# Attention output projection split into two halves by input, the latent half issued inside the differential attention

## The chip, the cores and the metric

The kernel runs on one core of a Trainium2 chip. The metric is the device time of one execution in microseconds (us). Before the change the median of three runs is 2091.11 us, between 2088.5 and 2091.54 us.

The core has a matrix engine (TensorE, PE in the profile), a vector engine (VectorE, DVE), a scalar engine (ScalarE, ACT), GpSimd (POOL) and a queue engine (SyncE, SP). Each runs its own list of instructions in order, and they wait for each other by semaphores. Matrix products land in PSUM, eight banks of 128 x 512 floats, called `banks` in the rows.

## The reference

Two layers of an encoder over 512 prompt rows and 32 sample rows (R = 544 rows together), width 2048. What matters here is the first layer:

```python
o_a = _diff_attention(qa, k_all.reshape(b, sk, H_A, 2, DQK), v_all, lam, q_chunk, k_chunk)   # 8 heads x 128
o_a = _rmsnorm(o_a, g_subln, SUBLN_EPS) * (1.0 - lam_init)
o_lat = _mla_attention(q_lat, q_pe, ckv_all, kpe_all, q_chunk, k_chunk)
o_b = jnp.einsum('bshc,chv->bshv', o_lat, w_uv)                                             # 8 heads x 128
o = jnp.concatenate([o_a.reshape(b, s, W_A), o_b.reshape(b, s, W_B)], axis=-1) * jax.nn.silu(gate)
return o @ w_out, new_rows
...
x = x + gate * y
```

The output projection `o @ w_out` takes 2048 inputs, of which the last 1024 come from the latent attention and the first 1024 from the differential attention. Layer 1 (a pooling mixer with its own projections) and a final norm follow.

## The kernel before

Data are kept transposed: 128 features on the partitions, 544 rows along the free dimension, so an activation of width 2048 is 16 slices of 128 x 544 (index k). Every float32 value that enters a large product is split into a rounded upper part and the remainder (`w_hi`, `w_lo`, `h_hi`, `h_lo`), and a product is three matmuls: hi x hi, hi x lo, lo x hi. Each is done for two column halves of 272 rows. One output tile of a projection (128 outputs) therefore takes 16 x 3 x 2 = 96 matmuls of 128 x 272 (`big_tile`, `tile_products`); 8 of the 16 slices take 48.

The program is a fixed sequence written by hand: layer 0 input projections, latent attention, differential attention, the norm of its heads, the output projection, then layer 1. Each engine has its own block, and loops that must match are written once in each. The tile counter g (G_OUT is the first tile of the output projection) numbers the weight tiles; SP loads tile g into slot g % 2 of `w_raw`, `split` on DVE (L1390) makes `w_hi` and `w_lo` from it, and PE waits for `split_ready`.

**Differential attention.** 36 units are taken in steps w (`d_unit`): nine to a pair of heads, 8 blocks of 128 queries with 1, 2, 3, 4, 4, 3, 2, 1 key blocks (w % 9 = 0 to 7) and one unit of the sample rows (w % 9 = 8). A unit goes PE scores (`d_scores`), DVE maximum (L1660, or L1656 for the sample rows), ACT exponential (L1241, L1234), DVE reciprocal, ACT scaling of the second map (L1256) one step later, DVE combination (L1687) two steps later, PE transposes (`d_turn`, L935) three steps later, then ACT upper part (`ptd_hi`, L1263) and DVE remainder (`ptd_lo`, L1709). In the step d_last + 4 the products with the values follow (`d_values`, 12 matmuls, and `d_sample_values`). Score banks are 0 to 3, two for even and two for odd steps; PE may run at most two steps ahead of the exponential. Turns and transposed values take banks 4 and 5 in turn, value products bank 6 and sample rows bank 7.

**Heads' norm.** ACT squares the eight heads, PE sums them over the partitions, ACT and DVE take the root and its reciprocal for 8 rows, PE spreads them over the partitions (`sel_row` products), DVE scales each head, and ACT and DVE split it into `h_hi` and `h_lo`. PE fills the wait for the reciprocal with the latent half (k = 8 to 15) of one projection tile, G_OUT.

**Output projection.** 16 tiles. For each, DVE also computes one tile of the layer 1 modulation (`ada_tile`: two multiply-and-reduce instructions over 128 x 2048, L1433), ACT loads the modulation weights of the tile after next from its own queue, evicts the tile from PSUM times the gate (`gated`, L1302), DVE adds it to `x` (`update`, L1744), ACT squares it, POOL adds the square to `ssq` (L634), and DVE splits the weights of the tile after next (L1395, L1396). `x` is read again from memory at the end of the heads' norm.

## Time and profile before

| | |
|---|---|
| runs before (three) | 2088.5, 2091.11, 2091.54 us |
| profiled execution | 2090.51 us, span 2088.7 us, mean granted TensorE clock 0.928 |
| PE / DVE / ACT / POOL busy | 1859.8 / 1278.0 / 406.5 / 174.2 us |
| differential attention | from 1010 to 1179 us of the span |
| heads' norm | 1179 to about 1217 us |
| output projection to the last addition to x | about 1217 to 1401 us |
| layer 1 and the final norm | 1401 to 2088.7 us |
| DMA | 307.05 MB, mean 147 GB/s |

The profile gives busy time of each engine, tenths of it in 40 slices of 52.2 us, the chain of work that ended last, and groups of instructions by line. Ends of matmuls are modelled; the distance between the starts of two matmuls is a better measure of what one costs. The granted clock is a share of 2.4 GHz.

### The profile page before, as it was taken

What the parts mean: (1) busy time and instruction counts of PE and PEld (TensorE: products, weight loads), DVE (VectorE), ACT (ScalarE), POOL (GpSimd) and SP (SyncE); (2) the same over time, 40 slices, a digit from 0 to 9 for tenths busy, and PEclk for the clock granted to TensorE, in tenths of its full rate; (3) what the DMA queues carried; (4) which work ended last, traced back from release to release, by engine and by line L of the source; (5) the groups of instructions that cost most, each with busy time, mean ns of one, the idle gap of its engine ahead of it and who ended that gap; (6) DMA issues with size and microseconds to landing.
All of it is one profiled execution on the core that took longest, in us unless ns stands there. A gap on an engine that the chain in (4) does not pass through costs nothing.

```text
span 2088.7 us, 32490 instructions
## 1 busy us (share of the span) xinstructions
PE 1859.8 (89%) x13182; PEld 1707.9 (82%) x13182; DVE 1278.0 (61%) x1598; ACT 406.5 (19%) x863; POOL 174.2 (8%) x101
## 2 busy tenths in 40 slices
PE   4539999999999978997767799987999999999995
PEld 0109999999999966776655599987999999999995
DVE  4898677677877653553455678887334444583444
ACT  1241000000000112332344421113111111131111
POOL 2770000000600000000000011110000000001110
PEclk8879999999999999998666799997999999999997
DMA  9565555445655432116221064431322333452222
GB/s 390 219 230 186 200 196 213 183 187 209 238 201 209 162 106 61 56 32 197 73 61 57 26 287 173 182 127 56 118 102 107 105 124 112 160 192 98 80 80 85
DMA packets 77395, 307.05 MB, mean 147 GB/s; under 512 B 11416, under 2 KB 19784, under 8 KB 49440
## 3 DMA queue, kind: packets, MB, share of 16 engines
q1 hardware_dynamic: 55792, 218.56, 28.6%
q10 hardware_dynamic: 20912, 86.71, 11.6%
q0 software_dynamic: 640, 1.10, 0.1%
q8 instruction: 32, 0.52, 0.1%
q14 instruction: 19, 0.16, 0.0%
HBM read 278.10 MB, written 28.24 MB: 147 GB/s over the span
## 4 chain that ended last, share of the span: by engine, by line
PE 74%; DVE 14%; ACT 4%; DMA 3%; issue 2%; POOL 2%; DVEq 0%; SPq 0%; ACTq 0%; POOLq 0%
PE banks L646 73%; DVE banks L1433 2%; POOL ssq L609 2%; DMA w_more<-in_w_ada_pe 1%; ACT pxd L1241 1%; DMA d_raw<-pool_d_scratch 1%; DVE std L1660 1%; DVE w_lo L1396 1%; DVE h_lo L378 1%; DMA w_adr<-in_w_ada_dve 1%; DVE rstd L1375 1%; DVE x L1854 1%; DVE ptd_lo L1709 0%; ACT px L1185 0%; DVE pt_lo L1602 0%
## 5 line engine op out<-in xcount | busy, mean ns | idle before, releaser
L646 PE MATMUL banks<-h_hi,w_hi 128*128 128x272 f32 x3712 | 774.4, 290 | 36.2 <-DVE h_lo L1414 15.1
L646 PE MATMUL banks<-h_hi,w_lo 128*128 128x272 f32 x3712 | 772.7, 290 | 0.0
L646 PE MATMUL banks<-h_lo,w_hi 128*128 128x272 f32 x3712 | 770.1, 289 | 0.0
L646 PEld LDWEIGHTS banks<-h_hi,w_hi 128*128 128x128 f32 x3712 | 588.0, 190 | 41.6 <-issue 19.0
L646 PEld LDWEIGHTS banks<-h_lo,w_hi 128*128 128x128 f32 x3712 | 588.0, 190 | 0.0
L646 PEld LDWEIGHTS banks<-h_hi,w_lo 128*128 128x128 f32 x3712 | 584.4, 190 | 0.0
L1433 DVE CUSTOM_DVE_ANT_0 banks<-w_adr,cond_b 128x2048 f32<-128x2048 f32 x160 | 387.0, 2419 | 18.9 <-DMA w_adr<-in_w_ada_dve 15.7
L1396 DVE TENSOR_TENSOR w_lo<-w_raw,w_hi 128x2048 fp32r<-128x2048 f32 x117 | 299.4, 2559 | 4.0
L1395 DVE CAST w_hi<-w_raw 128x2048 fp32r<-128x2048 f32 x117 | 145.2, 1241 | 225.1 <-PE banks L646 216.9
L634 POOL TENSOR_TENSOR ssq<-ssq,stage 128x544 f32<-128x544 f32 x32 | 48.1, 1502 | 1261.3 <-ACT stage L1054 1261.3
L1131 ACT ACTIVATE stage<-banks 128x544 f32<-128x544 f32 x48 | 30.2, 628 | 519.4 <-PE banks L646 519.4
L1744 DVE TENSOR_TENSOR x<-x,stage 128x544 f32 (+1 forms) x32 | 23.2, 726 | 136.6 <-ACT stage L1302 136.3
L1790 DVE TENSOR_TENSOR w<-u_ext 128x573 f32<-128x573 f32 x16 | 12.1, 756 | 138.8 <-ACT u_ext L1323 138.8
L1302 ACT ACTIVATE stage<-banks,mod 128x272 f32<-128x272 f32 (+2 forms) x96 | 32.5, 409 | 287.4 <-PE banks L646 163.6
L646 PE MATMUL banks<-w_more,cond_t 128*2 128x512 f32 x80 | 42.1, 682 | 35.1 <-DMA w_more<-in_w_ada_pe 21.0
L646 PEld LDWEIGHTS banks<-w_more,cond_t 128*2 128x2 f32 x80 | 6.9, 92 | 69.2 <-issue 42.9
L646 PE MATMUL banks<-w_raw,cond_t 128*2 128x512 f32 x48 | 30.1, 786 | 35.1 <-DMA w_raw<-in_w_ada_pe 35.1
L935 PE MATMUL banks<-id_t,pxd 128*128 128x128 f32 x80 | 21.4, 382 | 41.1 <-DVE pxd L1687 27.0
L646 PEld LDWEIGHTS banks<-w_raw,cond_t 128*2 128x2 f32 x48 | 4.4, 101 | 58.7 <-DMA w_raw<-in_w_ada_pe 32.5
L935 PEld LDWEIGHTS banks<-id_t,pxd 128*128 128x128 f32 x80 | 11.8, 184 | 45.4 <-DVE pxd L1687 29.1
L646 PE MATMUL banks<-cq,wq 128*128 128x272 f32 x128 | 32.9, 412 | 15.4 <-DVE cq L1531 9.0
L646 PEld LDWEIGHTS banks<-cq,wq 128*128 128x128 f32 x128 | 24.8, 199 | 22.2 <-issue 17.2
(288 smaller groups left out, 1675.9 us busy)
## 6 DMA issues: line engine op xcount, KB each, us to landing
w_adr<-in_w_ada_dve ACTq DMA_DIRECT2D x60, 1024.0 KB, 4.9
w_raw<-in_w_z SPq DMA_DIRECT2D x32, 1024.0 KB, 6.2
w_raw<-in_w_pin SPq DMA_DIRECT2D x32, 1024.0 KB, 4.8
w_adr<-in_w_ada_dve SPq DMA_DIRECT2D x20, 1024.0 KB, 4.9
w_raw<-in_w_gate SPq DMA_DIRECT2D x16, 1024.0 KB, 6.1
w_raw<-in_w_out SPq DMA_DIRECT2D x16, 1024.0 KB, 4.9
w_raw<-in_w_pout SPq DMA_DIRECT2D x16, 1024.0 KB, 4.8
w_more<-in_w_ada_pe SPq DMA_DIRECT2D x10, 1024.0 KB, 7.2
```

What stands on the lines that cost most here:

```text
L378: ins = eng.scalar_tensor_tensor(out=h_lo[:, k, r], in0=x[:, k, r], scalar=mod[:, c, k:k + 1], in1=h_hi[:, k, r].bitcast(F32), op0=ALU.add ...
L609: pool.tensor_tensor(ssq[:], ssq[:], (stage[:, 0], rstd[:])[k % 2], ALU.add).then_inc(sq_added, 1)
L634: pool.tensor_tensor(ssq[:], ssq[:], stage[:, s], ALU.add).then_inc(sq_added, 1)
L646: return pe.matmul(out, lhsT, rhs, start=start, stop=stop)
L935: m = pe.transpose(PS[:, 4 + j % 2, b * P:(b + 1) * P], pxd[:, w % 3, 0, b * P:(b + 1) * P], id_t[:])
L1131: act.activation(rows(stage[:, s]), acc[slot], func).then_inc(acc_free[slot], 1)
L1241: ins = act.activation(pxd[:, w % 3, e, 0:n], PS[:, 2 * (w % 2) + e, 0:n], ACT.Exp, bias=std[:, w, 2 + e:3 + e], scale=DIFF_SCALE, accum_o ...
L1302: ins = act.activation(stage[:, s, r], PS[:, 2 * slot + bank, cols], ACT.Identity, scale=mod[:, c, bass.ds(2 * t + (gate_tile + s), 1)])
L1395: vchain(dve, dve.tensor_copy(w_hi[:, slot], w_raw[:, slot]))
L1396: dve.tensor_tensor(w_lo[:, slot], w_raw[:, slot], w_hi[:, slot].bitcast(F32), ALU.subtract).then_inc(split_ready, 1)
L1433: ins = dve.tensor_tensor_reduce(ada_junk, w_adr[:, slot], cond_b[:, c, :], 1.0, 0.0, ALU.mult, ALU.add, ada_acc[:, c:c + 1])
L1744: dve.tensor_tensor(at(x, t2 + k), at(x, t2 + k), stage[:, slot], ALU.add).then_inc(x_new, 1)
```

## The change

The output projection becomes two series of half tiles. The latent half (inputs 1024 to 2047) of tiles 0 to 12 goes into the steps w = 0 to 38 of the differential attention, three steps to a tile, with 3, 3 and 2 of its 8 slices; tiles 13, 14 and 15 are put around the heads' norm. Each result is evicted by ACT times the gate, added to its slice of the input `x` by POOL, and written by ACT's queue to a scratch buffer in memory. The other half of each tile follows where the projection was, and adds to the `x` read back from that buffer. Weights are loaded in halves, and their upper part is now made by ACT (128 x 1024) instead of DVE (128 x 2048). The jobs of banks 4 and 5 are laid out in one table that now holds the value products too, which leaves banks 6 and 7 to the latent half.

```diff
+            def latent_half(n, ks):
+                g = G_OUT + n
+                if 0 in ks:
+                    pe.wait_ge(split_ready, g - G_KPE + 2)
+                    pe.wait_ge(acc_free[(g - 1) % 2], turn_of(g + 1))
+                for k in ks:
+                    m = half_products(6, g, k, HEADS + k, k == 0, k == HEADS - 1)
+                if HEADS - 1 in ks:
+                    m.then_inc(mm_done, 1)
             for w in range(D_UNITS + DLAG + 1):
                 if w < D_UNITS:
                     d_scores(w)
+                if w > DLAG and (w - DLAG - 1) % 9 == 8:
+                    d_sample_values((w - DLAG - 1) // 9)
                 for h in range(HEADS):
                     if w == v_step(h):
                         d_values_in(h)
-                if DLAG <= w < D_UNITS + DLAG:
-                    d_turn(w - DLAG)
+                if w < 3 * IN_STEPS:
+                    latent_half(w // 3, chunk_of[w % 3])
                 for h in range(HEADS):
                     if w == d_last(h) + DLAG + 1:
                         d_values(h)
-                if w - DLAG - 1 >= 0 and (w - DLAG - 1) % 9 == 8:
-                    d_sample_values((w - DLAG - 1) // 9)
+                if DLAG <= w < D_UNITS + DLAG:
+                    d_turn(w - DLAG)
+            latent_half(13, range(HEADS))
...
+            latent_half(14, range(HEADS))
+            latent_half(15, range(4))
...
# ACT
+            def half_hi(g, t2=0, t=0):
+                act.wait_ge(raw_in[g % 2], 16 * t + 16 * (g // 2 + 1 - ADA_PE // 2))
+                act.wait_ge(mm_done, t2 + (g - 1))
+                act.activation(half_slots(g)[0], w_raw[:, g % 2, 0:D // 2], ACT.Copy).then_inc(w_upper, 1)
+            def store_half(n):
+                act.wait_ge(x1_added, n + 1)
+                act.dma_start(x1_scr[n], x_half[n % 2][:]).then_inc(x1_out[n % 2], 16)
+            def evict_half(n):
...
+                for bank, cols, r, c in parts(R):
+                    ins = act.activation(y_half[n % 2][:, r], PS[:, 6 + bank, cols], ACT.Identity,
+                                         scale=mod[:, c, 2 * KT + n:2 * KT + n + 1])
+                ins.then_inc(acc_free[g % 2], 1)
...
+                if w < 3 * IN_STEPS and w % 3 == 2:
+                    if w // 3:
+                        store_half(w // 3 - 1)
+                    evict_half(w // 3)
+                if w % 3 == 0 and w and w // 3 + 1 <= IN_STEPS:
+                    half_hi(G_OUT + w // 3 + 1)
# POOL
+            for n in range(KT):
+                pool.wait_ge(x1_in[n % 2], 16 * (n // 2 + 1))
+                pool.wait_ge(x1_ev, n + 1)
+                pool.tensor_tensor(x_half[n % 2][:], x_half[n % 2][:], y_half[n % 2][:], ALU.add).then_inc(x1_added, 1)
# DVE
+            def half_lo(g, t2=0, t=0):
+                hi, lo = half_slots(g)
+                dve.wait_ge(w_upper, t2 + (g - G_OUT + 1))
+                dve.tensor_tensor(lo, w_raw[:, g % 2, 0:D // 2], hi.bitcast(F32), ALU.subtract).then_inc(split_ready, 1)
...
+                if w % 3 == 1 and w > 3 and w // 3 + 1 <= IN_STEPS:
+                    half_lo(G_OUT + w // 3 + 1)
...
+            with dve.Fori(0, KT // 2 - 2) as t:
+                dv.loop(t, 4)
                 for s in range(2):
                     ada_tile(ADA_P0 + ADA_P1 + s, 2 * t, t)
-                    update(G_OUT + s, 2 * t, t, 1, s, s)
-                    split(G_OUT + s + 2, 2 * t, t)
+                    update(G_O2 + s, 2 * t, t, 1, s, s)
+                    half_lo(G_O2 + s + 2, 2 * t, t)
```

In the new loop of the projection, `gated` on ACT does `half_hi` of the tile after next between the eviction and the square. SP issues the half loads, the slices of x, and the loads of heads and caches step by step in one list, and the condition vectors for `ada_tile` are loaded at the end of the attention steps instead of at the end of the heads' norm.

**PE, around step w % 9 = 7.** Before, the turn of unit w - 3 (L935) stands ahead of the value products (the rows with `ptd_hi` and `vr_hi`), which the sample scores (`kcs`) follow:

```order
L646 MATMUL banks<-kd_hi,qd_hi 128x128 x2
L646 MATMUL banks<-kd_hi,qd_lo 128x128 x2
L646 MATMUL banks<-kd_lo,qd_hi 128x128 x2
L646 MATMUL banks<-maskk_t,maskq_t 128x64 x2
L935 MATMUL banks<-id_t,pxd 128x128 x4
L646 MATMUL banks<-ptd_hi,vr_hi 128x512
```

Now the same scores, a chunk of three slices (L712 with `h_hi`, `w_hi`; the lower part of a latent half tile also lies in the tile called `w_hi`), the value products, and only then the turn (L1012):

```order
L712 MATMUL banks<-kd_hi,qd_hi 128x128 x2
L712 MATMUL banks<-kd_hi,qd_lo 128x128 x2
L712 MATMUL banks<-kd_lo,qd_hi 128x128 x2
L712 MATMUL banks<-maskk_t,maskq_t 128x64 x2
L712 MATMUL banks<-h_hi,w_hi 128x272 x2
...
L712 MATMUL banks<-h_hi,w_hi 128x272 x2
L712 MATMUL banks<-ptd_hi,vr_hi 128x512
...
L712 MATMUL banks<-ptd_lo,vr_hi 128x128
L1012 MATMUL banks<-id_t,pxd 128x128 x4
L712 MATMUL banks<-kcs,qds 32x272
```

The turn has moved behind 18 latent matmuls and 12 value matmuls of its step.

**ACT, step w % 9 = 5 and the next.** Between the split of the next head's queries and keys and the exponential of the next unit there now stand:

```order
L1333 ACTIVATE kd_hi<-kd 128x512
L1344 DMA x_half_scratch<-cos_t 128x544
L1353 ACTIVATE rstd<-banks,mod 128x272
L1353 ACTIVATE rstd<-banks,mod 128x240
L1353 ACTIVATE rstd<-banks,mod 128x32
L1357 ACTIVATE act_tmp<-act_tmp 1x1
L1381 ACTIVATE pxd,std<-banks,std 128x256 x2
```

L1344 is the store of the tile before, L1353 the eviction, which frees banks 6 and 7 for the next latent tile. Before, L1241 followed directly on L1219.

## Rows read from the trace of the kernel before

**Rows 1.** Page, granted clock in tenths in 40 slices of 52.2 us.

```profile
PEclk8879999999999999998666799997999999999997
```

**Rows 2.** Windows: us, PE, PEld, DVE, ACT, POOL busy (count), PEclk, DMA share, GB/s.

```profile
840.00:880.00 40.00, 38.43 (x192) 29.60 (x191) 20.96 (x56) 12.13 (x32) 0.00 (x0) 1.00 0.24 74
...
1092.00:1133.00 41.00, 29.03 (x165) 22.05 (x165) 23.75 (x63) 20.25 (x60) 0.00 (x0) 0.62 0.21 64
...
1189.40:1195.60 6.20, 6.20 (x49) 6.07 (x48) 4.25 (x2) 0.91 (x2) 0.00 (x0) 1.00 0.01 3
...
1255.00:1400.00 145.00, 144.38 (x1152) 144.16 (x1151) 124.16 (x100) 20.72 (x50) 17.91 (x12) 1.00 0.49 174
```

**Rows 3.** Waits from 1010 to 1180: us in total, times, longest.

```profile
ACT pxd L1241 <- DVE std L1661: 47.5, 28, 3.5
...
PE banks L935 <- DVE pxd L1687: 27.0, 14, 3.1
```

**Rows 4.** Chain that ended last: start us, us, what.

```profile
1066.26 1.24 DVE std L1660
...
1080.98 6.19 PE banks L646 x33
...
1098.38 4.34 PE banks L646 x20
...
1107.52 1.24 DVE std L1660
```

**Rows 5.** Timeline of PE in the heads' norm: start us, us, instruction.

```profile
1207.43 0.66 PE L646 MATMUL banks<-h_lo,w_hi 128*128 128x272 f32 x2
1207.88 0.66 PE L646 MATMUL banks<-h_hi,w_lo 128*128 128x272 f32 x2
```

**Rows 6.** Timeline of ACT around step 15 of the attention.

```profile
1075.94 0.62 ACT L1219 ACTIVATE kd_hi<-kd 128x512 fp32r<-128x512 f32 x1
1078.20 0.47 ACT L1241 ACTIVATE pxd<-banks,std 128x256 f32<-128x256 f32 x1 [1.64 <-DVE std L1661]
```

**Rows 7.** Timeline of DVE, one tile of the output projection.

```profile
1301.98 2.29 DVE L1433 CUSTOM_DVE_ANT_0 banks<-w_adr,cond_b 128x2048 f32<-128x2048 f32 x1
...
1306.86 0.17 DVE L1439 COPY mod<-ada_acc 128x2 f32 x1
1308.68 0.73 DVE L1744 TENSOR_TENSOR x<-x,stage 128x544 f32 x1 [1.65 <-ACT stage L1302]
1309.33 1.22 DVE L1395 CAST w_hi<-w_raw 128x2048 fp32r<-128x2048 f32 x1
1310.58 3.33 DVE L1396 TENSOR_TENSOR w_lo<-w_raw,w_hi 128x2048 fp32r<-128x2048 f32 x1
1313.83 2.29 DVE L1433 CUSTOM_DVE_ANT_0 banks<-w_adr,cond_b 128x2048 f32<-128x2048 f32 x1
```

**Rows 8.** Timeline of ACT and of POOL beside the same tile.

```profile
1307.51 1.02 ACT L1302 ACTIVATE stage<-banks,mod 128x272 f32<-128x272 f32 x3 [9.16 <-DVE ada_acc L1433]
...
1310.28 1.48 POOL L634 TENSOR_TENSOR ssq<-ssq,stage 128x544 f32<-128x544 f32 x1 [10.37 <-ACT stage L1054]
```

**Rows 9.** Timeline of DVE and of ACT at the head of the projection.

```profile
1210.27 2.29 DVE L1396 TENSOR_TENSOR w_lo<-w_raw,w_hi 128x2048 fp32r<-128x2048 f32 x1
...
1227.39 0.17 DVE L1439 COPY mod<-ada_acc 128x2 f32<-128x2 f32 x1
...
1216.36 3.64 ACT L1291 ACTIVATE cond_b<-cond_b 128x4096 f32<-128x4096 f32 x1 [6.73 <-DMA cond_b<-in_cB]
```

**Rows 10.** Timelines: last sample product on PE, last modulation and addition on DVE.

```profile
1179.11 0.40 PE L646 MATMUL banks<-ptds,vrs 32*128 32x32 f32 x2
...
1400.09 0.17 DVE L1439 COPY mod<-ada_acc 128x2 f32<-128x2 f32 x1
1400.53 0.72 DVE L1744 TENSOR_TENSOR x<-x,stage 128x544 f32<-128x544 f32 x1 [0.27 <-ACT stage L1302]
```

**Rows 11.** DMA issues by line: KB each, us to landing.

```profile
x<-in_xT SPq DMA_DIRECT2D x1, 3264.0 KB, 23.3
```

More of the change, by code:

```diff
@@ L66 @@
 G_OUT = G_GATE + GT
-G_PIN = G_OUT + KT
+G_O2 = G_OUT + KT
+G_PIN = G_O2 + KT
 G_GRP = G_PIN + 2 * KT
@@ L348, in program @@
         x_new = sem("x_new")
+        w_upper = sem("w_upper"); x1_ev = sem("x1_ev"); x1_added = sem("x1_added")
+        x1_in = [sem(f"x1_in{s}") for s in range(2)]
+        x1_out = [sem(f"x1_out{s}") for s in range(2)]
         d_ready = sem("d_ready"); d_stored = sem("d_stored")
@@ L560, in _ @@
             for s in range(2):
                 load_ada(s, w_ada_dve[ADA_P0 + ADA_P1 + s])
-            load_w(w_out[3], (G_OUT + 1) % 2, G_OUT + 3 - G_KPE)
-            sp.dma_start(x[:, 4:KT], xT[:, 4:KT]).then_inc(x_rest_in, 16)
-            with sp.Fori(0, KT // 2 - 2) as t:
+            for s in range(2):
+                load_half(w_out[s][:, 0:D // 2], G_O2 + s)
+            for s in range(2):
+                sp.wait_ge(x1_out[s], 16 * 6)
+            sp.dma_start(x[:, 0:12], x1_scr[0:12].rearrange("t p r -> p t r")).then_inc(x_in, 16)
@@ L565, in _ @@
+            for s in range(2):
+                sp.wait_ge(x1_out[s], 16 * KT // 2)
+            sp.dma_start(x[:, 12:KT], x1_scr[12:KT].rearrange("t p r -> p t r")).then_inc(x_rest_in, 16)
+            with sp.Fori(0, KT // 2 - 1) as t:
                 for s in range(2):
-                    load_w(tile_of(wo2, s, t + 2), (G_OUT + s) % 2, 2 * t + 4 + G_OUT - G_KPE + s)
+                    sp.wait_ge(split_ready, 2 * t + 2 + G_O2 - G_KPE + s)
+                    sp.dma_start(w_raw[:, (G_O2 + s) % 2, 0:D // 2],
+                                 tile_of(wo2, s, t + 1)[:, 0:D // 2]).then_inc(raw_in[(G_O2 + s) % 2], 16)
@@ L955, in d_sample_values, with half_products @@
                         last = j == KTS - 1
-                        m = small(PS[:, 7, P + NS * s:P + NS * s + NS], vrs[0:NS, 2 * t + s, :] if last else vcs[:, s, j, :],
+                        m = small(PS[:, bank, NS * s:NS * s + NS], vrs[0:NS, 2 * t + s, :] if last else vcs[:, s, j, :],
                                   ptds[0:NS, j, s, :] if last else ptds[:, j, s, :], j == 0, last)
                 m.then_inc(dfs_pv, 1)
+            def half_products(bank, g, k, h, first, last):
+                ks = slice(k * P, (k + 1) * P)
+                hi, lo = half_slots(g)
+                for i, (w, rows_of) in enumerate(((hi, h_hi), (hi, h_lo), (lo, h_hi))):
+                    for a in range(2):
+                        m = small(PS[:, bank + a, 0:HALF], w[:, ks], rows_of[:, h, a * HALF:(a + 1) * HALF],
+                                  first and i == 0, last and i == 2)
+                return m
+            def latent_half(n, ks):
[7 more added lines that the diff above has]
+                    m.then_inc(mm_done, 1)
             for w in range(D_UNITS + DLAG + 1):
@@ L1237, in _ @@
                         n = P * (i + 1)
-                        if w >= 3:
+                        if w >= 3 and w % 9 != 2:
                             act.wait_ge(df_tr, w - 2)
```

329 lines of the change are left out of this document (206 added, 123 removed).

## The prediction

> **What bounds the kernel now.** I read the granted clock by slices first [rows 1]. It is full for most of the program and falls to 0.6 or 0.7 in slices 20 to 23, the differential attention. Then the windows [rows 2]: in nine attention steps (41.0 us) PE is busy 29.0 us at a mean clock of 0.62, DVE 23.8 and ACT 20.3, so nobody is full. In the output projection (145 us) PE is busy 144.4 at clock 1.00, and DVE 124.2. The change moves 7.5 tiles' worth of matmuls out of the second stage into the gaps of the first.
>
> The waits of the attention stage say what those gaps are [rows 3]: ACT waits 47.5 us for DVE's scaled maximum, PE 27.0 us for DVE's combination of two maps. Step by step it is one loop between DVE and ACT (maximum, exponential, scaling, upper part of the turned map, its remainder, next maximum), with PE in it only at some places. The chain shows them in one period of nine steps, 1066.26 to 1107.52, 41.26 us: 6.19 us of value products and sample scores, then 4.34 us of value products [rows 4].
>
> The projection is closer to even than its busy shares look. DVE starts a tile at 1301.98 and the next at 1313.83: 11.85 us [rows 7]. Inside it DVE waits 1.65 us for ACT's eviction, and that eviction ended ACT's idle time of 9.16 us, whose releaser is DVE's modulation sum [rows 8]. So this is a DVE and ACT loop of 11.85 us that happens to be as long as PE's 96 matmuls (48 take 6.2 us at clock 1.00 [rows 2], so 12.4, a little less without the end). Halving PE's part alone would give nothing there; what counts is what leaves DVE.
>
> **The projection after.** One tile, from the start of the modulation on DVE: the addition to x can start at 6.70 and the next DVE instruction at 7.35, as now [rows 7]. ACT has finished the eviction at 6.57 (1307.51 + 1.02 - 1301.98 [rows 8]) and then makes the upper part, 128 x 1024. ACT copied 512 columns in 0.62 [rows 6] and did 4096 in 3.64 [rows 9], which gives 1.05 for 1024: done at 7.6, seen by DVE at 7.7. The remainder of 1024 columns, between 2.29 for 2048 [rows 9] and 0.73 for 544 [rows 7], is 1.2: 8.9. Then there is POOL: the same subtraction took 3.33 instead of 2.29 when POOL's addition began 0.3 us ahead of it [rows 7 to 9]. POOL's addition stays, once a tile, and will meet either this subtraction or the modulation, so I add the same 1.04: 9.95 us a tile. Low end 8.9 (POOL falls into a wait), high end 10.85 (below, rival three).
>
> The first and the last modulation copy stand at 1227.39 and 1400.09 [rows 9, 10], 172.7 us apart. After: 14 intervals of 9.95 and one that still holds the full split of the next projection's weights, 11.85, together 151.2. Gain 21.5 us. The bound on PE there, 48 matmuls in 6.2 us, is under 9.95. The two DMA streams grow shorter per tile, not longer.
>
> **The heads' norm.** PE's list gets tiles 13, 14 and 15 of the latent half instead of one half tile: 12.4 us more. About 3.6 us of them lie beside squares, root and reciprocal. In return the condition vectors are loaded at the end of the attention: ACT now waits 6.73 us for that load [rows 9], and DVE's first modulation, behind it in SP's list, comes late too. The Silu (3.64) still stands ahead of the first modulation. 12.4 - 3.6 - 6.7 = 2.1 us longer; ends -3 and +8. The read of x, 23.3 us for 3264 KB [rows 11], is issued right behind the weights at the end of the attention and has some 40 us to land, so it costs nothing; without that cover it could cost up to those 8 us.
>
> **The attention steps.** I follow one period with PE at full clock and ask for each addition whether something waits for it.
> - The remainder of the half weights (1.2 us on DVE) stands ahead of the next maximum in steps 4, 7 and 1 of each nine. In step 4 nothing covers it: +1.2. In 7 and 1 DVE then waits for PE anyway.
> - The eviction with the store ahead of it takes 0.65 for the issue (1306.86 to 1307.51 [rows 7, 8]), 1.02, and about 0.35 for the semaphore and the tiny copy: 2.0 us. In step 5 ACT is free 1.64 us between its splits and the next exponential [rows 6]: +0.35. In step 8 about 1.0 sticks out, since the sample step leaves ACT less.
> - New wait: the first chunk of a latent tile (w % 3 = 0) waits for banks 6 and 7, which that eviction frees. PE stops there, and queued behind it are 18 matmuls (2.3 us), the turn of unit w - 3, and the scores of w + 1. ACT wants that turn about 1.5 us after its exponential begins and gets it after 3.0. In step 6 this costs 1.2; in step 0 the load of the new head gives enough time.
> - Steps 7 and 8: the late turn delays the chunk of step 7, which now stands ahead of the value products, 1.4 us; the denser PE runs the 6.19 us piece faster, -0.7. Net +0.7.
> - Steps 2 to 4: value products, then the sample turn behind them, then sample values, a chunk of 2.3 us and only then the turn that ACT waits for. Against 1098.38 to 1107.52 today this is +1.8.
>
> Sum 6.25 us in a period. PE's load: today's 29.0 busy us would be 18.0 if all of it scaled with the clock; with 144 latent matmuls of 0.129 (18.6) that is 36.6 us, and 47.6 if none of it scaled. So against a period of 47.5 PE is nearly full, and it also has to stop three times for the eviction. I add 1.45 us for matmuls that still run at the lower clock: two 128 x 272 matmuls are 0.45 us apart there [rows 5], against 0.26 at 1.00. The period comes to 49.0, ends 43.3 (only step 4 and what sticks out of ACT is paid) and 54 (PE load 47.6 plus its stops). The steps from first to last maximum are 3.9 periods: 3.9 x 7.7 = 30.0. Two half tiles of weights are split before the first step (+2.5) and the last turn waits behind a chunk (+1.5): 34.0 us.
>
> New POOL additions (16, about 1.5 us each) can also hold DVE. In these steps most DVE work reads PSUM, and I leave them at nothing here; at 1.04 each, the price in the projection, they would be 13 us at most over 13 tiles. The Trainium skill (GPSIMD Engine Reference, Key points) says that GpSimd shares its SBUF interfaces with VectorE and contends with vector instructions in a two-port mode or with two SBUF inputs. The trace agrees for the subtraction of weights, 3.33 against 2.29, which has two SBUF inputs; by the rule the maxima and remainders from PSUM would be spared.
>
> **Sum.** 34.0 + 2.1 - 21.5 = +14.6 us on the profiled execution of 2090.5 us: 2105 us. Its own time is 0.6 us under the median of the three runs, so I use it as it is.
>
> **Rivals.**
> One, the filler is free. PE waits 27 us for DVE, which speaks for it, and the period becomes only 43.3: 4 + 7.8 + 2.1 - 21.5 = -7.6, 2083 us. It decides at a period of 45.0. Against it stand the order on PE (chunk ahead of the turn) and the new wait for the eviction.
> Two, the clock stays low in the attention steps. Then 18 latent matmuls take 4.1 us instead of 2.3, PE cannot do a step in 4.6 us, and the period is 54: 34.0 becomes 53.7, 2125 us. For it: the clock is 0.62 there with PE busy 71% of the time. Against: the latent attention at 96% busy has 1.00 [rows 2], and a PE that falls behind becomes denser. The Trainium skill (TensorE: Matmul & The Clock Gate, What's actually happening) states that the throttled state is the default and activity releases it; by that, filling the gaps would raise the clock and 1.45 us of my period would go, which is 2099 us in all. The two windows agree in direction only.
> Three, PE in the new projection falls to the low clock, because it is idle 3.8 us of each 9.95. A half tile is then 48 x 0.225 = 10.8 us, the tile 10.85, the gain 21.5 - 12.6 = 8.9: 2118 us.
> Four, the two stages cancel, period about 45: 2091 us.
>
> **How the numbers follow.** Forecast 0.42, its own range 2096 to 2115; rival one 0.25; two 0.15; three 0.08; four 0.10. A change under 0.2% (4.2 us) can't be told from none. Faster: rival one and a little of four, 0.27. Same: most of four and the edge of the forecast, 0.10. Slower: 0.63. The range 2080 to 2126 holds all four rivals' centres; about 1 in 10 lies below it (8.9 us a tile together with rival one would be 2068) and 1 in 10 above.
>
> **What would show it.** The nine-step period at 48 to 50 us instead of 41.26, PE busy over 85% of it at a clock near 0.9; PE waiting for the eviction at each third step; ACT waiting for turns, where now it waits for maxima alone. In the projection, tiles 9.9 to 10 us apart, PE busy near 60%, and DVE without idle time but the wait for the eviction. The first modulation copy 50 us after the last sample product (now 47.9 [rows 9, 10]). I am wrong if the period is under 45 us, or if tiles of the projection follow at 9 us or less.

## The result, and the profile after

| | before | after |
|---|---|---|
| median of four runs | 2091.32 us | 2157.39 us (2156.32 to 2158.31) |
| ratio, 95% interval | | 1.0317, 1.0299 to 1.0335 |
| profiled execution, span | 2090.51, 2088.7 us | 2156.32, 2154.5 us |
| first maximum of the attention | 1014.6 | 1020.3 |
| end of the last sample product | 1179.5 | 1253.4 |
| first modulation copy | 1227.4 | 1319.4 |
| addition of the modulation's bias | 1401.2 | 1467.9 |

The change costs 66 us. By the last three rows and the span (+65.8): the program up to the last product of the attention +73.9, the heads' norm +18.1, the projection -25.3, and the rest of the program -0.9. I had predicted +34.0, +2.1 and -21.5.

Page of after, busy tenths of PE and granted clock in the 40 slices (the clock answers [rows 1]):

```profile
PE   5549999999999969989787788775999999999995
PEclk8879999999999989987877787886999999999998
```

The clock of the attention slices has risen from 0.6 to 0.7 or 0.8, but there are more such slices. Windows of after (us, PE, PEld, DVE, ACT, POOL busy, PEclk, DMA share, GB/s): nine attention steps, the piece of them that ends the period, and the projection, against [rows 2]:

```profile
1093.00:1151.00 58.00, 46.85 (x310) 40.95 (x310) 28.16 (x66) 26.39 (x75) 4.04 (x3) 0.79 0.33 102
...
1137.00:1151.00 14.00, 13.35 (x67) 11.46 (x67) 3.15 (x9) 3.91 (x13) 1.33 (x1) 0.60 0.29 90
1320.00:1460.00 140.00, 106.40 (x672) 103.43 (x672) 113.38 (x101) 39.13 (x77) 24.75 (x15) 0.84 0.48 165
```

Nine steps take 58.2 us now. PE is busy 81% of them, so the filler has not filled it. In the last 14 us of this window it is busy 13.4 us, at a mean clock of 0.60, and DVE and ACT are busy only 3.2 and 3.9. Waits of the attention steps of after (us in total, times, longest), against [rows 3]:

```profile
DVE ptd_lo L1883 <- ACT ptd_hi L1403: 81.2, 32, 9.2
ACT pxd L1381 <- PE banks L1012: 72.3, 15, 10.2
PEld banks L712 <- issue: 46.5, 58, 7.0
ACT pxd L1381 <- DVE std L1836: 28.8, 17, 2.7
...
PE banks L712 <- ACT rstd L1353: 17.8, 4, 7.0
PE banks L712 <- ACT kpe L1353: 16.9, 5, 7.0
```

ACT's exponential (L1381) waited for DVE's maximum before, 47.5 us. It now waits 72.3 us for PE's turn (L1012). The reason is in the code of before as well: the exponentials have three buffers (`pxd[:, w % 3]`), so exponential w overwrites what turn w - 3 reads, and waits for it. The chain of after shows the lateness at two places, steps 15 and 21 (steps 6 and 3 of their periods), against [rows 4]:

```profile
1104.59 0.92 ACT kpe L1353 x3
1105.64 4.42 PE banks L712 x18
1110.06 0.83 PE banks L1012 x4
...
1138.23 10.54 PE banks L712 x45
...
1150.43 0.51 ACT pxd L1396
1151.13 0.29 DVE ptd_lo L1883
1151.42 1.14 DVE std L1835
```

At the first place the order is eviction of the latent tile (`kpe`), 18 latent matmuls, turn. Timeline of PE there:

```profile
1105.64 0.79 PE L712 MATMUL banks<-h_hi,w_hi 128*128 128x272 f32 x2 [6.96 <-ACT kpe L1353]
```

PE idles 6.96 us for the eviction, its clock falls from 1.00 to 0.50 in that time, and the 18 matmuls take 4.4 us where I had written 2.3. The second place is worse, and no eviction stands in it. Timeline of PE and ACT in step 21, the step behind the sample rows' turn:

```profile
1139.82 1.92 PE L712 MATMUL banks<-ptds,vcs 128*128 128x32 f32 x8
...
1142.23 1.92 PE L712 MATMUL banks<-ptds,vcs 128*128 128x32 f32 x8
...
1144.63 0.82 PE L712 MATMUL banks<-h_hi,w_hi 128*128 128x272 f32 x2
...
1148.62 0.27 PE L1012 MATMUL banks<-id_t,pxd 128*128 128x128 f32 x1
```

```profile
1148.98 0.69 ACT L1381 ACTIVATE pxd<-banks,std 128x512 f32<-128x512 f32 x1 [10.06 <-PE banks L1012]
```

Twenty products of the sample rows with the values (1139.82 to 1144.63, 4.8 us) and the chunk of 18 (to 1148.62, 4.0 us) stand ahead of a turn of one transpose, 0.27 us, and the exponential behind it waits 10.06 us. Before, the sample values stood behind the turn. PE does not wait for the eviction here: in the whole periods it waits for it 6.96 us in step 6 and 1.37 us in step 0, and nowhere else. Its clock is low all the same (window of after):

```profile
1131.00:1134.60 3.60, 1.81 (x11) 1.47 (x10) 2.71 (x8) 1.48 (x6) 0.00 (x0) 1.00 0.03 12
1134.60:1148.30 13.70, 13.05 (x58) 11.49 (x57) 4.69 (x14) 3.22 (x10) 1.33 (x1) 0.50 0.39 117
```

It fell at 1134.6, after PE had idled 1.79 us ahead of value products that waited for DVE's remainder.

The first maxima are a clock for each step. This table gives the time from the maximum of the step before to that of the step named (w % 9), in the first whole period, worked out from the starts of DVE's maxima, for the two kernels and four of the experiments below:

| step | 0 | 1 | 2 | 3 | 4 | 5 | 6 | 7 | 8 | sum |
|---|---|---|---|---|---|---|---|---|---|---|
| before | 2.93 | 5.25 | 2.63 | 4.90 | 4.63 | 4.16 | 6.86 | 3.57 | 6.35 | 41.3 |
| after | 2.92 | 7.88 | 3.77 | 5.45 | 11.52 | 5.29 | 6.84 | 8.33 | 6.29 | 58.3 |
| chunk last | 2.93 | 5.25 | 3.77 | 7.63 | 7.66 | 5.30 | 6.84 | 4.81 | 7.31 | 51.5 |
| slices 0, 4, 4 | 3.52 | 5.26 | 3.77 | 4.73 | 5.65 | 7.35 | 6.84 | 4.61 | 6.41 | 48.1 |
| one slice of eight | 2.92 | 5.26 | 3.77 | 4.79 | 5.66 | 5.28 | 6.86 | 4.60 | 8.35 | 47.5 |
| no latent, old banks | 2.93 | 5.62 | 3.77 | 3.82 | 6.07 | 5.29 | 6.84 | 4.71 | 6.29 | 45.3 |

Steps 1, 4 and 7 are those behind a first chunk: +2.6, +6.9, +4.8. Steps 2 and 5 have grown by 1.1 each. Periods of one kernel differ too: the second one is 58.1 in the kernel after, 49.6 with the chunk last and 46.7 in the last row, so differences of a period under 2 us are weak evidence.

The heads' norm, timelines of ACT and of SP of after:

```profile
1288.71 1.06 ACT L1339 ACTIVATE w_hi<-w_raw 128x1024 fp32r<-128x1024 f32 x1 [11.25 <-DMA w_raw<-in_w_out]
...
1300.18 0.66 ACT L1443 ACTIVATE h_hi<-od 128x544 fp32r<-128x544 f32 x1 [3.11 <-DVE od L1912]
1303.94 0.66 ACT L1443 ACTIVATE h_hi<-od 128x544 fp32r<-128x544 f32 x1 [3.11 <-DVE od L1912]
```

```profile
1275.03 1.94 SPq L575 DMA_DIRECT2D w_raw<-in_w_out x2
```

The first half weights of the new projection are issued last, behind the condition vectors and the modulation weights, and ACT waits 11.25 us for them. Then the heads come 3.76 us apart.

The projection, timeline of DVE, one tile of after against [rows 7]:

```profile
1350.75 0.72 DVE L1923 TENSOR_TENSOR x<-x,stage 128x544 f32 x1 [1.66 <-ACT stage L1467]
1351.57 1.22 DVE L1819 TENSOR_TENSOR w_lo<-w_raw,w_hi 128x1024 fp32r<-128x1024 f32 x1
1352.71 3.44 DVE L1600 CUSTOM_DVE_ANT_0 banks<-w_adr,cond_b 128x2048 f32<-128x2048 f32 x1
...
1356.24 2.30 DVE L1600 CUSTOM_DVE_ANT_0 banks<-w_adr,cond_b 128x2048 f32<-128x2048 f32 x1
...
1360.56 0.73 DVE L1923 TENSOR_TENSOR x<-x,stage 128x544 f32 x1 [1.65 <-ACT stage L1467]
```

9.81 us from one addition to x to the next (9.83 from one modulation copy to the next), against 11.85.

### The profile page after: what moved, and what is told of

Read it like the earlier page. It is cut to its first block, busy times and chain, and to the rows that moved or that the text cites. A ratio compares the mean times of both kernels' runs of the same rounds, so it can differ in the third digit from the quotient of the medians.

```text
span 2154.5 us, 32736 instructions
## 1 busy us (share of the span) xinstructions
PE 1892.2 (88%) x13182; PEld 1739.7 (81%) x13182; DVE 1269.0 (59%) x1598; ACT 454.0 (21%) x959; POOL 197.9 (9%) x117
## 4 chain that ended last, share of the span: by engine, by line
PE 71%; DVE 14%; ACT 6%; issue 3%; DMA 2%; POOL 2%; ACTq 0%; SPq 0%; DVEq 0%; POOLq 0%
PE banks L712 70%; DVE banks L1600 4%; POOL ssq L670 2%; DMA w_more<-in_w_ada_pe 1%; ACT pxd L1381 1%; ACT w_hi L1339 1%; DMA w_raw<-in_w_out 1%; DVE std L1835 1%; DVE h_lo L394 1%; DVE w_hi L1819 1%; ACT stage L1467 1%; DVE rstd L1542 0%; DVE x L2029 0%; DVE w_lo L1563 0%; ACT pxd L1396 0%
## 5 line engine op out<-in xcount | busy, mean ns | idle before, releaser
L712 PE MATMUL banks<-h_hi,w_hi 128*128 128x272 f32 x3968 | 840.6, 298 | 105.4 <-DVE w_lo L1819 34.2
L712 PE MATMUL banks<-h_lo,w_hi 128*128 128x272 f32 x3712 | 784.4, 294 | 0.0
L712 PEld LDWEIGHTS banks<-h_hi,w_hi 128*128 128x128 f32 x3968 | 642.8, 196 | 118.4 <-issue 93.3
L712 PE MATMUL banks<-h_hi,w_lo 128*128 128x272 f32 x3456 | 727.6, 293 | 0.0
L712 PEld LDWEIGHTS banks<-h_lo,w_hi 128*128 128x128 f32 x3712 | 602.8, 195 | 0.0
L712 PEld LDWEIGHTS banks<-h_hi,w_lo 128*128 128x128 f32 x3456 | 552.3, 193 | 0.0
L1600 DVE CUSTOM_DVE_ANT_0 banks<-w_adr,cond_b 128x2048 f32<-128x2048 f32 x160 | 402.2, 2514 | 18.7 <-DMA w_adr<-in_w_ada_dve 11.6
L1562 DVE CAST w_hi<-w_raw 128x2048 fp32r<-128x2048 f32 x101 | 125.6, 1243 | 215.2 <-PE banks L712 211.0
L1563 DVE TENSOR_TENSOR w_lo<-w_raw,w_hi 128x2048 fp32r<-128x2048 f32 x101 | 249.1, 2467 | 3.5
L695 POOL TENSOR_TENSOR ssq<-ssq,stage 128x544 f32<-128x544 f32 x32 | 49.6, 1550 | 790.5 <-ACT stage L1168 790.5
L712 PE MATMUL banks<-w_more,cond_t 128*2 128x512 f32 x80 | 43.7, 705 | 38.7 <-DMA w_more<-in_w_ada_pe 22.5
L712 PEld LDWEIGHTS banks<-w_more,cond_t 128*2 128x2 f32 x80 | 7.0, 94 | 74.0 <-issue 47.1
L1883 DVE TENSOR_TENSOR ptd_lo<-banks,ptd_hi 128x128 fp32r<-128x128 f32 (+3 forms) x32 | 15.7, 491 | 81.2 <-ACT ptd_hi L1403 81.2
L712 PE MATMUL banks<-w_raw,cond_t 128*2 128x512 f32 x48 | 28.9, 758 | 32.9 <-DMA w_raw<-in_w_ada_pe 32.9
L1381 ACT ACTIVATE pxd<-banks,std 128x128 f32<-128x128 f32 (+3 forms) x64 | 33.2, 523 | 101.1 <-PE banks L1012 72.3
L712 PEld LDWEIGHTS banks<-w_raw,cond_t 128*2 128x2 f32 x48 | 4.2, 97 | 55.8 <-DMA w_raw<-in_w_ada_pe 30.6
L712 PE MATMUL banks<-cq,wq 128*128 128x272 f32 x128 | 34.3, 426 | 14.2 <-DVE cq L1698 9.0
L701 POOL TENSOR_TENSOR cos_t<-cos_t,kpe 128x544 f32<-128x544 f32 x8 | 10.8, 1347 | 388.1 <-ACT act_tmp L1357 388.1
```

What stands on the lines that cost most here:

```text
L695: pool.tensor_tensor(ssq[:], ssq[:], stage[:, s], ALU.add).then_inc(sq_added, 1)
L712: return pe.matmul(out, lhsT, rhs, start=start, stop=stop)
L1381: ins = act.activation(pxd[:, w % 3, e, 0:n], PS[:, 2 * (w % 2) + e, 0:n], ACT.Exp, bias=std[:, w, 2 + e:3 + e], scale=DIFF_SCALE, accum_o ...
L1562: vchain(dve, dve.tensor_copy(w_hi[:, slot], w_raw[:, slot]))
L1563: dve.tensor_tensor(w_lo[:, slot], w_raw[:, slot], w_hi[:, slot].bitcast(F32), ALU.subtract).then_inc(split_ready, 1)
L1600: ins = dve.tensor_tensor_reduce(ada_junk, w_adr[:, slot], cond_b[:, c, :], 1.0, 0.0, ALU.mult, ALU.add, ada_acc[:, c:c + 1])
```

## The experiments

All start from the changed kernel. The period is that of the table above. Each batch of runs had the kernel before beside it, with medians from 2090.1 to 2093.1 us, and the ratios are to those; so times of different batches compare only to about 3 us.

| edit | median us | ratio to before, 95% | period |
|---|---|---|---|
| chunk last in the step | 2127.11 | 1.0149 to 1.0190 | 51.5 |
| fourth buffer for exponentials | 2133.04 | 1.0182 to 1.0216 | 51.3 |
| slices 0, 4, 4 | 2124.83 | 1.0144 to 1.0178 | 48.1 |
| early loads in the norm | 2149.31 | 1.0259 to 1.0293 | 58.3 |
| chunk last and slices 0, 4, 4 | 2138.42 | 1.0202 to 1.0255 | 54.2 |
| chunk last, slices 0, 4, 4, fourth buffer, early loads | 2122.06 | 1.0123 to 1.0173 | 51.3 |
| one slice of eight | 2117.38 | 1.0095 to 1.0148 | 47.5 |
| small splits | 2141.24 | 1.0207 to 1.0263 | 54.1 |
| turn before values | 2151.68 | 1.0253 to 1.0294 | 57.9 |
| turn before values, slices 0, 4, 4 | 2123.62 | 1.0128 to 1.0162 | 47.8 |
| one slice, turn before values | 2117.48 | 1.0099 to 1.0133 | 48.6 |
| early loads, spread products first | 2142.13 | 1.0217 to 1.0253 | 58.3 |
| one slice, small splits | 2110.98 | 1.0063 to 1.0117 | 46.3 |
| slices 0, 4, 4, splits on GpSimd | 2120.68 | 1.0115 to 1.0183 | 48.4 |
| best without GpSimd | 2103.83 | 1.0037 to 1.0078 | 47.0 |
| best with GpSimd | 2099.99 | 1.0024 to 1.0049 | 45.3 |
| no latent in the steps, old banks | 2108.15 | 1.0057 to 1.0087 | 45.3 |
| best, sample values after the turn | 2100.30 | 1.0026 to 1.0053 | 45.2 |

**The chunk behind the turn.**

```diff
-                if w < 3 * IN_STEPS:
-                    latent_half(w // 3, chunk_of[w % 3])
                 for h in range(HEADS):
                     if w == d_last(h) + DLAG + 1:
                         d_values(h)
                 if DLAG <= w < D_UNITS + DLAG:
                     d_turn(w - DLAG)
+                if w < 3 * IN_STEPS:
+                    latent_half(w // 3, chunk_of[w % 3])
```

> One edit to the changed kernel: in each attention step PE issues the latent chunk last, behind the value products and the turn. Theory A (the turn stands behind the chunk, and the exponential of the next use of the buffer waits for it): the 81.2 us of DVE waiting for the turned map and most of the 97 us of ACT waiting for turns shrink, the period of nine steps falls from 58.2 us to 49 to 52, the time to about 2125 to 2133 us. Theory B (PE is full: its own matmuls at a low clock set the period, wherever they stand): the period stays at 56 or more and the time at 2150 or more. Theory C (the extra work of ACT, DVE and POOL sets the period): also unchanged.

30 us less, in the range of theory A. Not one matmul was taken away, so the place of the chunk alone is worth that, and theories B and C fail as the main cause. Steps 1 and 7 are nearly back to before; steps 3 and 4 are not (7.63 and 7.66 against 4.90 and 4.63). ACT's waits for turns fall from 72.3 to 21.5 us.

**A fourth buffer.**

```diff
-                        if w >= 3 and w % 9 != 2:
-                            act.wait_ge(df_tr, w - 2)
+                        if w >= 4:
+                            act.wait_ge(df_tr, w - 3)
```

> One edit to the changed kernel: a fourth buffer for the exponentials, so that the exponential of step w waits for the turn of unit w - 4 and not of w - 3. The order on PE stays. Theory A1 (the wait of the exponential itself carries the loss): the waits of 10 us in step 3 go and the period falls by about 8 us, the time to about 2125. Theory A2 (the turn is late for whoever wants it: the exponential gets free but the upper part and the remainder of the turned map wait for the same turn, and the next maximum stands behind them): the period falls by 0 to 4 us, the time stays at 2140 to 2157. Theory B and C (PE or the other engines are full): unchanged.

24 us less, 7.0 in the period, between the ranges of theories A1 and A2. The order on PE is that of the changed kernel, so this run singles out the wait that my prediction had left out: the exponential's, for its buffer. What remains of the lateness falls on the upper part. Timeline of ACT in this kernel, step 21: it waits 5.19 us, where the exponential had waited 10.06.

```profile
1126.81 0.69 ACT L1383 ACTIVATE pxd<-banks,std 128x512 f32<-128x512 f32 x1 [1.72 <-DVE std L1838]
1133.94 0.28 ACT L1405 ACTIVATE ptd_hi<-banks 128x128 fp32r<-128x128 f32 x1 [5.19 <-PE banks L1014]
```

**No chunk in the first step.**

```diff
-        chunk_of = ((0, 1, 2), (3, 4, 5), (6, 7))
+        chunk_of = ((), (0, 1, 2, 3), (4, 5, 6, 7))
```

> One edit to the changed kernel: the eight slices of a latent tile are taken as 0, 4 and 4 in its three steps instead of 3, 3 and 2, so that the eviction of the tile before has a whole step, and no matmul waits for it. Theory A with weight on the eviction: PE's 35 us of waiting for the eviction go (nine waits of 7.0 us), the period falls by 5 to 8 us, the time to about 2125 to 2137. Theory A with weight on the place of the chunk alone: 24 matmuls now stand ahead of the turns of two steps in three, 18 and 12 before, so the period stays within 2 us, 2150 to 2160. Theory B: unchanged or a little less.

33 us less, 10.2 in the period, a little past the range. The edit takes the chunk out of steps 0, 3 and 6 and with it the wait for the eviction, so it does not price the two apart; in step 3, which shrinks from 11.5 to 5.7 us (the interval to step 4), PE had not waited for the eviction at all. (The nine waits were not of 7.0 us each, as I wrote ahead of the run: four are of 5.9 to 7.0, five of 1.3 to 2.5.) Windows of this kernel and of the one with one slice of eight (seven left out):

```profile
1079.00:1127.00 48.00, 42.17 (x309) 36.95 (x309) 27.80 (x66) 26.42 (x75) 4.03 (x3) 0.89 0.39 122
```

```profile
1078.00:1125.00 47.00, 31.80 (x183) 24.70 (x181) 27.53 (x66) 26.13 (x75) 4.00 (x3) 0.68 0.39 123
```

126 matmuls more in a period, and it is 0.6 us longer. Placed like this they are nearly free: PE is busy 42 us instead of 32, at clock 0.89 instead of 0.68.

**Both places.** The two edits together.

> Both edits at once: the chunk last in the step, and the slices taken as 0, 4 and 4. Alone they gave 2127.1 and 2124.8 us, 30 and 33 less than the changed kernel's 2157.4, periods near 50.6 and 48.0. Theory A (one serial loop: eviction, chunk, turn, exponential; either edit cuts it at another place): the two gains overlap in most of their sum, time 2115 to 2122, period 46 to 47.5. Rival (two separate costs that add): 2157 - 63 = about 2094, period near 42. Theory B (PE's own load then sets the period): no further gain, 2123 to 2127.

Wrong for all three: slower than either alone. With 24 matmuls last in a step, the next scores stand behind them and behind value products that wait for DVE's remainder (20.6 us in four waits). Step 8 takes 10.09 us instead of 6.41, step 3 takes 7.63. One more run with the fourth buffer and the early loads:

> Chunk last, slices as 0, 4, 4, the fourth buffer for exponentials, and the early loads of the first half weights. If the fourth buffer has nothing left to free once the turn comes early, this is the kernel with both places less 8 us for the loads, about 2110. If the remaining loss is still a wait for turns, 2100 or less. It would have to fall under 2087 to beat the kernel before.

2122.06, above both figures that I had named. The chunk's place is a balance: ahead of the turn it delays ACT, at the end of the step it delays the maximum.

**What PE's part costs.** Seven of eight slices left out in the steps.

```diff
-        chunk_of = ((0, 1, 2), (3, 4, 5), (6, 7))
+        chunk_of = ((), (), (7,))
```

> The changed kernel with seven of the eight slices of each latent half tile left out in the attention steps (13 tiles x 42 matmuls, 546 in all); the eighth slice stands in the third step of the tile. Splits, evictions, additions, loads and stores stay, so this prices PE's part. Theory A and B (PE's matmuls and what waits for them are the loss): the period falls from 58.2 to 43 to 46 us, the time to about 2097 to 2110. Theory C (what was added on ACT, DVE and POOL is most of it): the period stays above 50, the time above 2125.

40 us less, the period 47.5 where I expected 43 to 46, between theories A and C. So 10.8 us of the 17.0 go with these matmuls, and 6.2 stay without them. Then the splits, of 128 instead of 1024 columns:

```diff
-                    half_hi(G_OUT + w // 3 + 1)
+                    half_hi(G_OUT + w // 3 + 1, cols=P)
-                    half_lo(G_OUT + w // 3 + 1)
+                    half_lo(G_OUT + w // 3 + 1, cols=P)
```

> The changed kernel with the splits of half weights in the attention steps cut from 1024 to 128 columns on ACT and DVE (11 tiles, each about 0.9 us less on ACT and 1.0 us less on DVE); the other columns are not split. By the terms of my sum (1.2 us in one of three steps, the others beside waits) the period falls by 1 to 2 us, the time by 4 to 8 us, 2149 to 2153. If the splits stand on the loop in each of the three steps, 3 to 6 us a period, 2133 to 2145. If the loop eviction, chunk, turn and exponential hides them: 0 to 2 us.

16 us less, 4.2 in the period: the splits do stand in the loop. By the intervals of this run 2.3 of it lie in steps 2, 5 and 8, whose maxima follow DVE's remainder (2.84, 4.82 and 5.36), and most of the rest in step 4 (10.28). What part ACT's half has in that is not shown.

**The order of the value products.**

```diff
                 for h in range(HEADS):
                     if w == d_last(h) + DLAG + 1:
                         d_values(h)
```

goes behind `d_turn`, with the table of banks in the same order; on the changed kernel, on slices 0, 4, 4 and on the kernel with one slice.

> One edit to the changed kernel: the turn goes ahead of the value products (as it stood before the change), and the latent chunk stays ahead of both. Two steps of nine have value products. Theory E (a second part of the loss is this order: the values wait for the remainder of the last map, with the turn and so ACT queued behind them): the period falls from 58.2 by 3 to 6 us, the time to 2133 to 2146. Rival (the chunk ahead of the turn is the whole loss of order): 0 to 1 us a period, 2152 to 2157.

> Slices as 0, 4 and 4 (alone 2124.8 us, period 48.2) together with the turn ahead of the value products. Theory E: the period falls to 43 to 46 us, the time to 2104 to 2117. Rival (with PE relieved, what was added on ACT and DVE sets the period): within 1 us of 48.2, 2121 to 2126. Warning from the run with both places, whose two gains turned into a loss of 11 us: an edit may also move a wait into a worse step.

> The kernel with one of eight latent slices in the attention steps (seven left out; 2117.4 us, period 47.6) with the turn ahead of the value products. What is left over the 41.26 us of before is then the work added on ACT, DVE and POOL alone. Theory E: the period is 43 to 45 us, time 2099 to 2108: the additions cost 2 to 4 us, the order of values 3 to 4. Theory C: the period stays at 47 or more, and 6 us of each period belong to ACT, DVE and POOL.

2151.68, 2123.62 and 2117.48: theory E falls three times. The order gives 6 us in the first kernel and nothing that can be told from zero in the others.

**The heads' norm.**

```diff
+            load_half(w_out[0][:, 0:D // 2], G_O2)
             ...
+            load_half(w_out[1][:, 0:D // 2], G_O2 + 1)
             sp.dma_start(cond_b[:], ...
-            for s in range(2):
-                load_half(w_out[s][:, 0:D // 2], G_O2 + s)
```

> One edit to the changed kernel: the first two half tiles of weights of the second half are loaded ahead of the condition vectors and the modulation weights, and a slice of x behind them. Theory D (the 11.25 us in which ACT waits for that load lie on the path of the heads' norm): the first modulation copy comes 8 to 11 us earlier after the last sample product than the 66 us now, the time falls to about 2147 to 2149. Rival (the Silu waits for the condition vectors or x anyway, or the spread products at the low clock take the time): 0 to 3 us.

The time is 8.1 us less, the stretch from last sample product to first modulation copy 61.7 instead of 66.0, between theory D and the rival. The wait of 11.25 us has gone; 4.3 of it was on the path, since the heads' chain took its place. Of the 6.6 us between the two profiled spans, 2.1 lie behind the projection, and I can't say where from; the rest of the 8.1 is within what batches differ by.

```diff
-            widen(2)
-            widen(3)
+            for h in range(2, HEADS):
+                widen(h)
...
-                if k + 4 < HEADS:
-                    widen(k + 4)
```

> The kernel with the early loads of the half weights (2149.3 us), and in the heads' norm the products that spread the reciprocal over the partitions all stand ahead of the first tile's products, not between its slices. Theory F (each head now waits 3.76 us for six products and two spread products at half clock): the heads 4 to 7 come at 1.6 to 2.0 us instead of 3.76, the first modulation copy 6 to 9 us earlier, the time about 2140 to 2143. Rival (the Silu or x sets the start of the projection, or the first eviction now waits for PE): 0 to 3 us, 2146 or more.

7.2 us less, the stretch 54.8 us, theory F. Timeline of ACT in this kernel, the last heads 1.8 us apart:

```profile
1294.43 0.66 ACT L1440 ACTIVATE h_hi<-od 128x544 fp32r<-128x544 f32 x1 [1.16 <-DVE od L1909]
1296.24 0.66 ACT L1440 ACTIVATE h_hi<-od 128x544 fp32r<-128x544 f32 x1 [1.16 <-DVE od L1909]
```

**What the other 6 us are.**

> One of eight latent slices in the attention steps (seven left out) and splits of half weights of 128 instead of 1024 columns there (the rest not split). With the slices alone left out the period was 47.6, the time 2117.4. Theory C1 (the splits stand open on both ACT and DVE, 1.9 us in each third step, and are the larger part of what the other engines add): period 42.0 to 43.2, time 2096 to 2101. Theory C2 (eviction, addition and the new order weigh more): period 44 or more, time 2104 or more.

Period 46.3: only 1.2 less than with the slices alone left out, as C2 has it, and the second period is as long as there, 47.5. Of the 6.4 us in time 4.6 lie ahead of the first maximum (1015.6 instead of 1020.2). In the intervals of this run steps 2 and 5 did fall to 2.84 and 4.36, but step 3 rose to 6.33. Why is not shown: value products that wait for DVE's remainder stand ahead of the sample rows' turn (21.1 us in seven waits), but they wait as long in the kernel with one slice (20.8). The splits moved to GpSimd:

```diff
+                    pool.tensor_copy(hi, w_raw[:, g % 2, 0:D // 2]).then_inc(w_upper, 1)
+                    pool.wait_ge(w_upper, n + 3)
+                    pool.tensor_tensor(lo, w_raw[:, g % 2, 0:D // 2], hi.bitcast(F32), ALU.subtract).then_inc(split_ready, 1)
```

> Slices as 0, 4 and 4 (2124.8 us, period 48.2), and GpSimd makes both parts of the half weights of tiles 2 to 13 in the attention steps, where it was idle 90 per cent of the time. Theory C1 (ACT and DVE lose 5 us a period to the splits): period 43 to 45, time 2106 to 2114. Rival (GpSimd slows DVE by sharing memory, or PE then sets the period): 46 or more, 2117 or more.

2120.68, 4 us less than without, the period unchanged: the rival. Its four runs lie between 2117.9 and 2131.3 us, so even the 4 us are not sure; in the profiled run the first maximum comes 4.2 us earlier (1015.8) and the steps take as long as before.

> The changed kernel with the latent products of tiles 0 to 12 left out of the attention steps altogether, and with them gone the value products have bank 6 and the sample rows bank 7 to themselves, in the order turn, value products, sample values, as before the change. Splits, evictions (read from SBUF), additions, loads and stores stay. With one slice of eight left and the shared banks the period was 47.6. Theory G (the one table for banks 4 and 5, by which turns and value products wait for each other's readers, is the rest): period 42.5 to 44.5, time 2097 to 2105. Theory C (work on ACT, DVE and POOL is the rest, whatever the banks): period 46.5 or more, 2112 or more.

Between the theories: 45.3 and 2108.15. Old banks and order, and the last slice gone, are worth 2.2 us of this period against the run with one slice, and 4.0 remain with no latent matmul in the steps. Over all steps, from first to last maximum, the three kernels take 176.2, 171.0 and (before) 153.5 us, which over 3.9 periods makes it 1.3 and 4.5 a period. Most of the 4.0 can be read off. Timeline of DVE and of POOL in the kernel with one slice, step 15 (w % 9 = 6):

```profile
1090.47 1.19 DVE L1836 TENSOR_SCALAR std<-std 128x2 f32<-128x2 f32 x1
```

```profile
1090.31 1.33 POOL L701 TENSOR_TENSOR cos_t<-cos_t,kpe 128x544 f32<-128x544 f32 x1 [17.16 <-ACT act_tmp L1357]
```

The scaling of two numbers takes 0.17 us elsewhere and about 1.2 here, beside POOL's addition. It stands between maximum and exponential, and step 7 is longer than before by 1.0 to 1.2 in each of the four experiments of the table. With DVE's split in steps 2 and 5, 2.3, that is 3.3 of the 4.0.

**Versions to beat the kernel before.** Slices 0, 4, 4, fourth buffer, early loads, spread products first; then with the splits on GpSimd; then with the sample values behind the turn.

> Slices as 0, 4 and 4, the fourth buffer for exponentials, the early loads and the spread products ahead of the first tile. By the sum of the parts: 2124.8 - 8 (loads) - 7 (spread) = 2110, less what the fourth buffer gives beside the slices, 0 to 8 us: 2102 to 2110. It stays slower than the kernel before if the splits are what is left.

> All of it: slices as 0, 4 and 4, fourth buffer, early loads, spread products first, and the splits on GpSimd. By the sum of the parts 2102 to 2110 less 11 to 19 us: 2085 to 2098, about equal to the kernel before (2091). If GpSimd's sharing with DVE eats the gain, 2100 or more.

> The kernel with all five edits (2100.0 us), and the products of the sample rows with the values behind the turn of their step, not ahead of it. The exponential after the sample step waited 3.75 us for this turn in the kernel with slices 0, 4, 4 alone. Theory G': the period falls by 1.5 to 3 us, the time to 2088 to 2094, equal to the kernel before or a little under. Rival (with four buffers for exponentials this wait is covered already): 2098 to 2101.

2103.83, 2099.99 and 2100.30. The best is 57 us faster than the changed kernel and still slower than before, by a ratio of 1.0024 to 1.0049. In it the steps up to the last sample product take 28 us more than before, the norm 7 more, and the projection 25 less. The last edit gave nothing, as its rival said.

## Why the prediction was wrong

**The failed step** is "New wait" of the attention steps, and the term for steps 2 to 4 that rests on it. I followed the chain eviction, first chunk, turn, and wrote that "ACT wants that turn about 1.5 us after its exponential begins", which is its use for the upper part. ACT wants it before the exponential begins, to have the buffer. So whatever stands ahead of a turn on PE also stands ahead of an exponential and of the next maximum, in one serial loop. The fourth buffer, which takes this one wait away, gave back 7.0 us of a period. The eviction is a link of the loop in steps 6 and 0 only. In step 3, the costliest, it is 20 sample products and the chunk, 8.8 us at a clock of 0.50, where my term for steps 2 to 4 came to 1.8 in all; no run moves the sample products alone in the changed kernel, so their share is not shown apart. I took 1.2 us in step 6, nothing in step 0 ("the load of the new head gives enough time"), and 1.8 for steps 2 to 4. By the table, the steps behind them grew by 4.8, 2.6 and, for 3 and 4 together, 7.4. With 0.7 for steps 7 and 8 and 1.45 for the low clock, my terms of PE's order were 5.2 us. Measured are 13.8: all growth of steps 1, 3, 4 and 7, less the 1.0 of POOL.

**Lower split:** 1.2 in step 4, and "in 7 and 1 DVE then waits for PE anyway". The maxima behind steps 4 and 1 both came 1.1 later; only behind 7 is there no growth, and even there the interval fell by 0.9 with small splits. 2.3 instead of 1.2.

**POOL's additions:** left at nothing, with 1.04 each as the bound. One of three in a period met the scaling, for 1.04. I had looked at maxima and remainders and not at the small instruction between them.

**Eviction sticking out of ACT:** 1.35. No row shows such a cost beside the loop; ACT waits for DVE at that time (in the kernel with slices 0, 4, 4 it waits 1.55 us in step 6, right after the eviction).

So 58.2 instead of 49.0. From first to last maximum the kernel takes 61.5 us more than before, where I had 30.0. Ahead of the first maximum it is 5.7 instead of 2.5, and behind the last one 6.7 instead of 1.5; what makes up these two was not looked into. My upper end for the period, 54, was made from PE's load, and the loop is longer than that load, since PE idles in it 19% of the time.

**Rivals one and two:** the filler was far from free as it was placed; with slices 0, 4, 4 PE's part nearly is, and the period is still 48.1, since the other engines' part is not. As to the clock, the period passed 54, but not because PE was full: it was busy 81%. At the chunk of step 6 the clock was low behind 6.96 us of idling for the eviction; in step 3 it fell after PE had been busy 1.8 of 3.6 us, ahead of the work of both. The Trainium skill's statement (TensorE: Matmul & The Clock Gate, What's actually happening) that activity releases the throttle agrees with 0.62 before and 0.89 with the slices placed as 0, 4, 4; it did not help where PE had to wait.

**The heads' norm:** +18.1 instead of +2.1, past my end of +8. Three terms failed. I counted what the earlier loads of the condition vectors save, and not that SP's list puts the half weights behind them: 4.3 us by the run with early loads. And I counted the added tiles' matmuls, and not that spread products are interleaved with a tile's slices at half clock, 3.76 us a head: 6.9 by the run with the spread first. 6.9 stay with both edits. The 6.7 that I took off was right: ACT's wait for the condition vectors is gone, and the Silu starts behind its table load (1.0 later for the upper part of a half tile that now stands ahead of it), and DVE's first modulation no longer waits for its weights, 2.4 more. What was too small is PE's 12.4 - 3.6 = 8.8: in the run with the spread first the last head still comes 14.9 us later after the last sample product than before (43.1 instead of 28.2). Why is open.

**The projection was right:** 9.83 us a tile where I had 9.95, with POOL's collision on the modulation (3.44 instead of 2.30) and not on the subtraction. The gain is 25.3 and not 21.5: 1.7 from 14 tiles at 9.83, and 1.8 from the last interval, where I had let 11.85 stand and it took 10.1. Rival three did not come: PE is busy 76% (I had written near 60%) at clock 0.84, and DVE still sets the tile. Reading x back cost nothing: no instruction of the projection waits for it.

## What to carry to other kernels

Before work is put ahead of an instruction in an engine's list, list every waiter of that instruction, the ones that want its buffer as well as those that want its result, and add the piece to each loop it closes. "Engine idle 30% of the time" says how much work fits, and not where: here 126 matmuls of a period cost 10.8 us in one order and 0.6 in another. And a small instruction on the critical loop deserves the same look for contention as a large one.

## What the hardware showed that I had not expected

A 128 x 2 scaling in SBUF on DVE took 1.2 us instead of 0.17 beside one GpSimd addition of 1.33 us. In every run with these additions this scaling, when it starts during a GpSimd addition, cast or subtraction, ends 0.02 to 0.03 us before that instruction does: 1.2 us when it starts 0.16 us into an addition, 0.58 when it starts 0.81 into one. It is not DVE as a whole that is held: the 128 x 1 scaling with `lam_w` (L1852) kept its 0.21 us beside such additions. The Trainium skill (GPSIMD Engine Reference, Key points) names two-port modes as well as two SBUF inputs as what contends; this scaling has one SBUF input, so by that rule it would be of the first kind, which no row names. GpSimd makes the upper part of 128 x 1024 in 1.04 us in most tiles (splits on GpSimd), as fast as ACT, and the remainder in 2.4 to 2.7 where DVE takes 1.22.
